# A fused projection's start: scale weights in two halves, the second half's rows behind the third chunk, more turns of the unit matrix

## What is computed

```python
def modulation(cond, w_mod, b_mod):
    m = jax.nn.silu(cond) @ w_mod + b_mod
    shift, scale, gate = jnp.split(m, 3, axis=-1)
    return shift, scale, gate

# reference
shift, scale, gate = modulation(c, w_mod[l], b_mod[l])
shift_c, scale_c, gate_c = modulation(c_ctx, w_mod[l], b_mod[l])
h = rmsnorm(x, norm_g[l]) * (1 + scale[:, None]) + shift[:, None]
hc = rmsnorm(ctx, norm_g[l]) * (1 + scale_c) + shift_c
p = h @ w_in[l]            # its first 768 columns are q (512), k (128), v (128)
```

## Time and profile before

| | |
|---|---|
| median of three runs | 1354.84 us |
| the profiled execution | 1355.44 us, of which the span 1353.6 us |
| PE busy | 98% |
| DVE, ACT, POOL busy | 71%, 43%, 46% |
| mean DMA rate over the span | 105 GB/s |
| first projection matmul | 21.42 us |

### The profile page before, as it was taken

How to read it: one execution, slowest core, us unless ns; L and a number is a source line. 1 busy time by engine, 2 the same in 40 slices (tenths; PEclk the granted TensorE clock), 3 DMA queues, 4 the chain that set the end, 5 groups by cost and what they waited for, 6 DMA issues and landing times.

```text
span 1353.6 us, 22599 instructions
## 1 busy us (share of the span) xinstructions
PE 1328.2 (98%) x7798; PEld 901.0 (67%) x7798; DVE 960.4 (71%) x1463; ACT 586.0 (43%) x1118; POOL 625.7 (46%) x314
## 2 busy tenths in 40 slices
PE   7999999999999999999999999999999999999998
PEld 5789775555555555555555554688888788878886
DVE  3598878877787777787787787542233745999986
ACT  3565335445445445445445447241313132333332
POOL 0443239998888899888888885100000010000000
PEclk9999999999999999999999999999999999999999
DMA  9867445111110111111101110943434066424431
GB/s 362 289 183 214 123 137 161 39 32 29 37 31 29 37 32 31 37 31 30 36 31 31 35 31 5 291 152 109 132 140 151 21 218 233 141 93 156 154 126 63
DMA packets 77287, 142.64 MB, mean 105 GB/s; under 512 B 7581, under 2 KB 42533, under 8 KB 75818
## 3 DMA queue, kind: packets, MB, share of 16 engines
q1 hardware_dynamic: 68746, 124.89, 28.1%
q0 software_dynamic: 7760, 16.78, 4.4%
q10 hardware_dynamic: 720, 0.15, 0.1%
HBM read 112.30 MB, written 29.50 MB: 105 GB/s over the span
## 4 chain that ended last, share of the span: by engine, by line
PE 85%; DVE 5%; issue 1%; ACT 1%; DMA 1%; SPq 0%; DVEq 0%; POOL 0%; POOLq 0%; ACTq 0%
PE pv_ps L1637 18%; PE ring_ps L1621 10%; PE ring_ps L1622 9%; PE acc L63 8%; PE acc L64 8%; PE acc L65 8%; PE ring_ps L1565 6%; PE o_ps L63 2%; PE o_ps L64 2%; PE o_ps L65 2%; PE q_ps L63 1%; PE q_ps L65 1%; PE q_ps L64 1%; PE ring_ps L1645 1%; DVE y L2294 1%
## 5 line engine op out<-in xcount | busy, mean ns | idle before, releaser
L1347 POOL TENSOR_TENSOR prob_sum<-prob_sum,prob 128x1024 f32<-128x1024 f32 x217 | 528.1, 2434 | 83.9 <-DVE prob_sum L1472 60.9
L1451 DVE TENSOR_REDUCE chunk_max<-ring_ps 128x1 f32<-128x512 f32 x496 | 307.4, 681 | 84.4 <-PE ring_ps L1565 83.2
L1386 ACT ACTIVATE prob<-ring_ps 128x512 f32<-128x512 f32 x576 | 290.0, 634 | 70.9 <-PE ring_ps L1622 70.6
L1637 PE MATMUL pv_ps<-prob,v 128*32 128x512 f32 x2304 | 260.7, 595 | 0.2 <-DVE att L1467 0.2
L1621 PE MATMUL ring_ps<-blk_q_hilo,k_hi 128*128 128x512 f32 x576 | 234.5, 407 | 2.6 <-ACT prob L1386 1.8
L1622 PE MATMUL ring_ps<-blk_q_negm,k_lo 68*128 68x512 f32 x576 | 227.6, 395 | 0.0
L1637 PEld LDWEIGHTS pv_ps<-prob,v 128*32 128x32 f32 x2304 | 68.2, 109 | 150.0 <-issue 134.1
L63 PE MATMUL acc<-hh,w_rest_hi 128*128 128x512 f32 x384 | 151.1, 394 | 0.7 <-DVE hl L98 0.7
L64 PE MATMUL acc<-hl,w_rest_hi 128*128 128x512 f32 x384 | 150.4, 392 | 0.0
L65 PE MATMUL acc<-hh,w_rest_lo 128*128 128x512 f32 x384 | 150.3, 391 | 0.0
L1621 PEld LDWEIGHTS ring_ps<-blk_q_hilo,k_hi 128*128 128x128 f32 x576 | 109.5, 190 | 51.4 <-DVE blk_q_negm L1233 13.8
(11 more groups left out here) (386 smaller groups left out, 2225.2 us busy)
## 6 DMA issues: line engine op xcount, KB each, us to landing
xt_raw<-in_xt SPq DMA_DIRECT2D x16, 512.0 KB, 5.2
x_tok<-in_x SPq DMA_DIRECT2D x16, 512.0 KB, 5.3
blk_q_max<-q_scratch SPq DMA_DIRECT2D x64, 128.0 KB, 2.6
blk_q_hilo<-q_scratch SPq DMA_DIRECT2D x32, 256.0 KB, 2.7
h_raw<-in_xg SPq DMA_DIRECT2D x4, 2048.0 KB, 8.7
rest_scratch<-stage SPq DMA_DIRECT2D x32, 256.0 KB, 2.3
rows<-in_x SPq DMA_DIRECT2D x16, 512.0 KB, 4.2
out_x<-rows SPq DMA_DIRECT2D x15, 512.0 KB, 2.6
```

The lines of the kernel that those rows point to most:

```text
L1347: nc.gpsimd.tensor_tensor(acc_pool[slot][:], acc_pool[slot][:], prob[j][:], ALU.add).then_inc(s_psum, 1)
L1386: nc.scalar.activation(prob[j][:, e * QB:(e + 1) * QB], score_bank(t)[:], ACT.Exp).then_inc(s_exp, 1)
L1451: nc.vector.reduce_max(chunk_max[:, q, c:c + 1], ring[banks[c]][:], X_AXIS).then_inc(s_mfree, 1)
L1637: last = nc.tensor.matmul(pv_ps[row:row + QUAD], k.v[:, 2 * j + e, kvh, half * QUAD:(half + 1) * QUAD], prob[j][:, e * QB:(e + 1) * QB], s ...
```

## The change

The scale weights come in two halves of 512 columns each (`w_scale[0]`, `w_scale[1]`), that is the scale of chunks 0 to 3 and of chunks 4 to 7. They lie where the shift weights will lie later, and no longer under the raw weights, so weight loads wait for nothing and the shift loads wait for the rows of the half that they overwrite. The half `b` takes two loads of 1 MB (four chunks of 512 columns each). Its rows (`scale_rows(b)`) are 32 matmuls of 128 columns, its turn is one, and `scale_columns(b)` makes four chunks' scale columns. The first half is made at the start, with nine turns of the unit matrix between its two bursts; the three turns ahead of the first turn of rows go. The second half's rows stand behind chunk 2, its turn behind tile 0's part of chunk 3, its columns on VectorE between the low parts of chunks 3 and 4 and ahead of the second halves of the x parts. Shift rows of pairs 0 and 1 stand behind chunk 6, those of pairs 2 and 3 behind chunk 7. Tile 2's x columns are loaded ahead of shift loads 2 and 3.

The diff, with the bodies of the shift rows' turn and columns left out, which do what they did:

```diff
--- before.py
+++ after.py
@@ -234,7 +234,8 @@
         b_part = place("b_part", [P, W], F32, work_at)
-        w_scale = place("w_mod_scale", [P, KD, D], F32, k.key_at)
+        w_scale = [place("w_mod_scale0", [P, KD, D // 2], F32, k.value_at),
+                   place("w_mod_scale1", [P, KD, D // 2], F32, AT_CTX_W)]
         w_raw = place("wqkv_raw", [P, KD, W], F32, k.key_at)
@@ -256,6 +257,7 @@
         row_ps = mod_ps[0]
+        scale_ps = (mod_ps[0], trq_ps)
         q_negm0, q_max0, chunk_max, neg_max = k.q_negm[0], k.q_max[0], k.chunk_max, k.neg_max
@@ -266,7 +268,7 @@
-        s_pad, s_cond, s_used = S("cond_pad_zeroed"), S("cond_ready"), S("w_scale_used")
+        s_pad, s_cond = S("cond_pad_zeroed"), S("cond_ready")
         s_mrow, s_mrow_sb, s_cols = S("mod_and_bias_rows_done"), S("mod_rows_copied"), S("mod_cols_done")
@@ -311,14 +313,11 @@
             def load_shift(i):
-                sp.wait_ge(s_used, 3)
-                if i == 3:
-                    sp.wait_ge(s_mrow, 1)
+                sp.wait_ge(s_mrow, i // 2 + 1)
                 sp.dma_start(w_shift[i // 2][:, i % 2 * 2:i % 2 * 2 + 2, :],
             def load_w(c):
-                sp.wait_ge(s_used, (1, 1, 2, 2, 2, 3, 3, 3)[c])
                 sp.dma_start(w_raw[:, c, :], w_in_v[:, c, 0:W]).then_inc(s_wr[c], 16)
@@ -338,30 +337,37 @@
 
-            for i in range(4):
-                sp.dma_start(w_scale[:, 2 * i:2 * i + 2, :], w_mod_v[:, 2 * i:2 * i + 2, D:2 * D]).then_inc(s_mod[i], 16)
+            def load_scale(i):
+                b, half = divmod(i, 2)
+                part = slice(half * KD // 2, (half + 1) * KD // 2)
+                sp.dma_start(w_scale[b][:, part, :],
+                             w_mod_v[:, part, D + b * (D // 2):D + (b + 1) * (D // 2)]).then_inc(s_mod[i], 16)
+
+            load_scale(0)
+            load_scale(1)
             load_xt(0)
+            load_w(0)
             load_xt(1)
-            for c in range(4):
+            load_w(1)
+            load_w(2)
+            load_scale(2)
+            load_scale(3)
+            for c in range(3, KD):
                 load_w(c)
             load_shift(0)
-            load_w(4)
-            load_w(5)
             load_shift(1)
-            load_w(6)
-            load_w(7)
+            load_xt(2)
             load_shift(2)
...
             load_x(1)
-            load_xt(2)
             load_xt(3)
...
                 load_x(m)
-            sp.wait_ge(s_mrow, 2)
+            sp.wait_ge(s_mrow, 3)
             sp.dma_start(c_raw[:], w_in_v[:, :, ATTN_W:W]).then_inc(s_wc, 16)
@@ -543,27 +549,31 @@
             act.wait_ge(s_mrow, 1)
-            nc.scalar.activation(mod_row[0][:], mod_ps[0][:, 0:256], ACT.Copy).then_inc(s_mrow_sb, 1)
-            for m in range(2):
-                x_high(m, slice(0, 4))
+            nc.scalar.activation(mod_row[0][:, 0:P], scale_ps[0][:, 0:P], ACT.Copy).then_inc(s_mrow_sb, 1)
+            x_high(0, slice(0, 4))
             act.wait_ge(s_scale, 2)
             w_high(0)
-            w_high(1)
+            x_high(1, slice(0, 4))
+            for c in range(1, 4):
+                w_high(c)
             for m in range(2):
                 x_high(m, slice(4, 8))
-            for c in range(2, KD):
+            act.wait_ge(s_mrow, 2)
+            nc.scalar.activation(mod_row[0][:, P:2 * P], scale_ps[1][:, 0:P], ACT.Copy).then_inc(s_mrow_sb, 1)
+            act.wait_ge(s_scale, 4)
+            for c in range(4, KD):
                 w_high(c)
-            act.wait_ge(s_mrow, 2)
+            act.wait_ge(s_mrow, 3)
             nc.scalar.activation(mod_row[1][:], mod_ps[1][:, 0:256], ACT.Copy).then_inc(s_mrow_sb, 1)
             x_high(2)
-            act.wait_ge(s_mrow, 3)
+            act.wait_ge(s_mrow, 4)
             nc.scalar.activation(b_part[:, 0:512], trq_ps[:], ACT.Copy)
-            act.wait_ge(s_mrow, 4)
+            act.wait_ge(s_mrow, 5)
             nc.scalar.activation(b_row[:, 0:512], trq_ps[0:SDK, :], ACT.Copy).then_inc(s_browhi, 1)
@@ -832,32 +842,43 @@
 
-            def mod_columns(out, i, bias):
-                cols = mod_ps[i][:, 256:512].rearrange("p (f i r) -> p f i r", f=2, i=4)
+            def scale_columns(b):
+                dve.wait_ge(s_cols, b + 1)
+                cols = scale_ps[b][:, 256:256 + P].rearrange("p (i r) -> p i r", i=4)
+                part = slice(b * KD // 2, (b + 1) * KD // 2)
                 for side in range(2):
-                    last = nc.vector.tensor_tensor(out[:, side, :].rearrange("p (i f) -> p f i", f=2),
+                    last = nc.vector.tensor_tensor(k.scale[:, side, part], cols[:, :, side],
+                                                   vecs[:, 3 * KD + b * KD // 2:3 * KD + (b + 1) * KD // 2], ALU.add)
+                last.then_inc(s_scale, 1)
+                dve.wait_ge(s_scale, 2 * b + 1)
+                gains_of = vecs[:, 4 * KD + b * KD // 2:4 * KD + (b + 1) * KD // 2]
+                nc.vector.scalar_tensor_tensor(k.scale[:, :, part], k.scale[:, :, part], 1.0,
+                                               gains_of.unsqueeze(1).broadcast_to([P, 2, KD // 2]), ALU.add,
+                                               ALU.mult).then_inc(s_scale, 1)
+
...
 
-            dve.wait_ge(s_cols, 1)
-            mod_columns(k.scale, 0, 3).then_inc(s_scale, 1)
-            dve.wait_ge(s_scale, 1)
-            nc.vector.scalar_tensor_tensor(k.scale[:], k.scale[:], 1.0,
-                                           vecs[:, 4 * KD:5 * KD].unsqueeze(1).broadcast_to([P, 2, KD]), ALU.add,
-                                           ALU.mult).then_inc(s_scale, 1)
-            for m in range(2):
-                x_low(m, slice(0, 4))
+            scale_columns(0)
+            x_low(0, slice(0, 4))
             dve.wait_ge(s_scale, 2)
             w_low(0)
-            w_low(1)
+            x_low(1, slice(0, 4))
+            for c in range(1, 4):
+                w_low(c)
+            scale_columns(1)
             for m in range(2):
                 x_low(m, slice(4, 8))
-            for c in range(2, KD):
+            dve.wait_ge(s_scale, 4)
+            for c in range(4, KD):
                 w_low(c)
-            dve.wait_ge(s_cols, 2)
-            mod_columns(k.shift, 1, 2).then_inc(s_shift, 1)
+            dve.wait_ge(s_cols, 3)
+            shift_columns().then_inc(s_shift, 1)
             dve.wait_ge(s_shift, 1)
@@ -949,24 +970,42 @@
 
-            def mod_rows(i, w, c, cw):
-                for j in range(4):
-                    last = nc.tensor.matmul(mod_ps[i][32 * j:32 * (j + 1), 0:256], cond_pad[:, c, :],
-                                            w[:, cw, j * 256:(j + 1) * 256], start=(c == 0), stop=(c == KD - 1))
-                return last
-
-            def mod_turn(i):
-                pe.wait_ge(s_mrow_sb, i + 1)
+            def keep_running(count):
+                for i in range(count):
+                    nc.tensor.transpose(trk_ps[:, 0:P], k.ident[:], k.ident[:])
+
+            def scale_rows(b):
+                for c in range(KD):
+                    if c % (KD // 2) == 0:
+                        if b == 0 and c:
+                            pe.wait_ge(s_const, 32)
+                            keep_running(9)
+                        pe.wait_ge(s_mod[2 * b + c // (KD // 2)], 16)
+                    for j in range(4):
+                        last = nc.tensor.matmul(scale_ps[b][32 * j:32 * (j + 1), 0:P], cond_pad[:, c, :],
+                                                w_scale[b][:, c, j * P:(j + 1) * P], start=(c == 0), stop=(c == KD - 1))
+                last.then_inc(s_mrow, 1)
+
+            def scale_turn(b):
+                pe.wait_ge(s_mrow_sb, b + 1)
+                nc.tensor.transpose(scale_ps[b][:, 256:256 + P], mod_row[0][:, b * P:(b + 1) * P],
+                                    k.ident[:]).then_inc(s_cols, 1)
+
...
@@ -1009,33 +1048,26 @@
             pe.wait_ge(s_cond, 1)
-            for i in range(4):
-                pe.wait_ge(s_mod[i], 16)
-                for c in (2 * i, 2 * i + 1):
-                    last = mod_rows(0, w_scale, c, c)
-                last.then_inc(s_used if i < 3 else s_mrow, 1)
-            def keep_running(count):
-                for i in range(count):
-                    nc.tensor.transpose(trk_ps[:, 0:P], k.ident[:], k.ident[:])
-
-            pe.wait_ge(s_const, 32)
-            keep_running(3)
-            mod_turn(0)
+            scale_rows(0)
+            scale_turn(0)
             keep_running(13)
             for c in range(KD):
-                if c % 4 == 0:
-                    pe.wait_ge(s_xlo, 2 + c // 2)
                 pe.wait_ge(s_wlo, c + 2 if c else 1)
                 for n in range(2):
+                    if c % 4 == 0:
+                        pe.wait_ge(s_xlo, n + 1 + c // 2)
                     q_chunk(n, c)
...
                     kv_chunk(n, c)
-                if c == 5:
+                    if c == 3 and n == 0:
+                        scale_turn(1)
```

(44 more changed lines are left out.)

## The result

| | before | after |
|---|---|---|
| median of 21 runs each | 1358.46 us | 1360.72 us |
| lowest | 1354.59 | 1357.08 |
| ratio to before | | 1.0025 [1.0017, 1.0034] |
| profiled execution (span) | 1355.44 (1353.6) | 1361.35 (1359.5) |

The change makes the kernel slower by 0.25%, about 3.4 us by the ratio (by its interval 2.3 to 4.6). One of the 21 runs after took 2632.81 us and is left out of the ratio; the median of the other 20 is 1360.46. The 3.4 us lie within the 0.3% named in the prediction, and the measured time lies outside its range, 1352.8 to 1357.2. The kernel before also reads higher over 21 runs than over the three shown at first: 1358.46 against 1354.84. So 3.6 us of the miss in absolute time are the baseline. With it even an unchanged kernel would have come out above the range.

The account below looks back on a forecast made before the run. TensorE, 98% busy, bounds the kernel. Chunk 0's 6.0 us gain goes to loads and stalls: T 0.8 later; chunk 7 ahead saves 1.6, the second chain eats 0.7: -0.1, so 1354.7 us, range 1352.8 to 1357.2.

Parts of the forecast that it names:

- the 0.3% named in the prediction: Whole kernel: 4.06 us, about what a measurement tells from no change; slower by more 0.04, faster by more 0.02.
- T: Start: moment when all shift rows are done, 40.21 us before, forecast 41.0, 0.8 later.
- rival (a): Chunks 0 to 2 and 4: low clock, 4.24 instead of 2.12 us a chunk; ends 1356.3 or 1358.4 us; chance 0.16.
- chunk 3 lands at 22.3: Loads at the start: weight chunk 3 lands at 21.9 plus 0.1 for each of four short-row loads.
- the two loads of the second half: DMA queue ahead of weight chunk 3: 5.16 us at 407 GB/s, plus 0.1 each for short rows.
- My bound for the four loads: Scale weight loads with 2 KB rows: nothing to +1.0 us on chunk 3's landing at 21.9.
- rival (c): Start: short rows at bound or second half's rows 3.9 us; tile 2 +0.6 to +1.2 us, 1355.7; chance 0.10.
- handed on one for one: Behind 46 us: all hangs on PE's progress, so the start's gain or cost reaches the end unchanged.
- Taken off the median of 1354.84: Whole kernel: the 0.1 us gain subtracted from the median before gives 1354.7 us.
- their bound: Short-row scale loads: 0.25 us more per 1024 KB, from context weights with 1 KB rows at 371 GB/s.
- (b): Second half's chain or PE's stall shorter: tile 2 at 44, -2.0 us, 1352.8; chance 0.12.

Follow-up runs that it names:

- Experiment 2: The changed kernel with weight chunk 3 loaded ahead of both scale loads of the second half; 1358.44 us, ratio 1.0015 to the kernel before.
- 11: The changed kernel with all three reordering edits, plus twenty turns of the unit matrix ahead of tile 2; 1359.52 us, ratio 1.0014 to the kernel before.
- 3: The changed kernel with the second half's rows copied ahead of the second x parts and turned ahead of chunk 3; 1357.54 us, ratio 1.0006 to before.
- 5: The changed kernel with three edits: weight chunk 3 loaded first, second half's turn first, tile 2's parts first; 1356.28 us, ratio 0.9999 to before.
- experiment 8: The changed kernel without the nine turns between the two bursts of the first half; 1360.84 us, ratio 1.0025 to the kernel before.
- experiment 1: The changed kernel again, no edit; 1360.01 us, ratio 1.0026 to the kernel before.
- experiment 12: The kernel before again, no edit; 1356.23 us, ratio 0.9998 to its other runs.
- experiment 7: The kernel before with each scale load cut into two of 512 columns (2 KB rows), same order; one execution, profiled run 1360.12 us.
- 9: The kernel before with ten turns of the unit matrix ahead of tile 2; 1359.15 us, ratio 1.0016 to the kernel before.
- 10: The kernel before with twenty turns of the unit matrix ahead of tile 2; 1360.87 us, ratio 1.0024 to the kernel before.
- 6: The changed kernel with turns of the unit matrix (16 and 13) filling PE's idle time ahead of chunks 3 and 4; 1359.26 us, ratio 1.0020 to before.
- 4: The changed kernel with tile 2's high part between the squares and its low part ahead of the variance; 1359.95 us, ratio 1.0022 to before.

## Why the prediction went wrong

**Right, by its own steps.** Chunk 0 was earlier by 6.7 us (forecast 6.0) and loads took it back. Chunk 3 was released by its low part, PE idled 1.6 us ahead of chunk 4 (2) and 0.67 ahead of tile 2 (0.7), released by the low part of x. From T to tile 2 it took 47.08 - 42.09 = 4.99 us (4.95). From chunk 3's start to chunk 4's it took 4.08 us (4.15), and to T 42.09 - 25.46 = 16.63 (16.65). Chunk 0 ran at the upper level, so rival (a) in the form in which I stated it, a clock that is low in the chunks, didn't come about. That chunk 0 was earlier than forecast is luck in part: in this profile the second burst of scale rows was already at the upper level, and where it wasn't (experiments 2 and 11) chunk 0 started at 15.4 and 15.7 us. The traces speak for turns that count as work: in three profiles (after, 3 and 5) the clock rose at 10.43, 10.61 and 9.99 us, when PE had done one burst and then only the nine turns, while in the old start one burst and a gap were followed by three more bursts before it rose, during turns. The Trainium skill, "TensorE: Matmul & The Clock Gate", Part 4: PE-mode transpose, has it that a transpose doesn't count as PE being busy; these rises disagree with it, while experiment 8 by itself decides nothing.

**The failed step: "chunk 3 lands at 22.3".** It landed at 23.4 (23.2 to 23.5 in the six profiles with this order of loads). Every later instant is late by this amount: chunk 3 by 1.11, T by 1.09, tile 2 by 1.13. Experiment 2 moves weight chunk 3 out from behind the two scale loads (it lands at 16.95) and gives back 1.2 us at 65 us, which shows the cause. The term of the sum that was mis-sized is that of the two loads of the second half, 5.16 us and 0.2 for their short rows: they took 6.29 us. The first half's second load accounts for the other 0.2 us (10.67 where I had 10.26 and 0.2). Short rows explain little: 1 MB took 2.70 us in steady running where I had 2.68, so 5.4 for the two. The other 0.9 us is a load that lands late by itself. In after the third load landed 3.66 us behind weight chunk 2 (19.79 against 16.13) and the fourth 2.63 behind it, in experiment 1 the third took 2.69 us and the fourth 3.69. In all nine profiles with the new start one of the two took 2.6 to 2.7 us and the other 3.1 to 4.0, the third in five of them, and the fourth in four. The DMA engines weren't idle meanwhile: 393 GB/s over the 7.27 us between the landings of weight chunks 2 and 3 are 2.86 MB, and the three loads that landed hold 2.49. The bytes weren't extra ones either, since both kernels had moved the same 15.87 MB when `cos_k`, the next table in the queue, landed, at 42.79 us before and at 43.46 after. So bytes of later loads went ahead while one load waited for its last part. The old order has such a load too: its second shift load took 2.95 us instead of 2.56 (3.27 in experiment 12), where nobody waited for it. What holds the load up is open. My bound for the four loads was +1.0 on 21.9; measured is +1.5, beyond it. The times are those of rival (c), which I had given 0.10.

**The second failed step: "handed on one for one".** It was read off the busy share, and PE 100% busy from 110 to 205 us does hand a delay on: 1.6 us stay 1.6. But the lag had grown from 1.05 at 46 us to 1.6 at 124 us at two waits for VectorE (0.94 us idle where before had 0.72), where the share is 51.17 of 53 us. These steps appear in the versions with the new start and not in experiments 7, 9, 10 and 12, which have the old one; why VectorE falls back there isn't shown. Beyond 207 us the executions at a clock of 0.998 and more add some 0.6 us (2.2 against 1.6). In the profiles of after and of experiments 9 and 10 that is the wait near 1120 us; it isn't shown that it is so in all.

**The baseline.** "Taken off the median of 1354.84" was a third failing: three runs, two of them at the low end of its spread, stood for a kernel whose median over 21 is 3.6 us higher. That alone put the range too low.

**Not foreseen: the clock in the attention.** Falls to half level at 209, 232 and 850 us come in some executions; the two in the profile after cost 2.5 + 1.0 us, more than the change loses at the start. They strike the old order too (experiment 7). I found no instruction of the change that causes them; filling PE's idle time (6) or not (1), and delay by itself (9: one run of 12 at 0.994; 10, 11: no run below 0.995), don't settle why the changed kernel had the lowest ones. Sorted afterwards, the clock was 0.994 or less in 11 of 64 runs of the kernels whose chunk 3 waits for the late load and whose columns come late (after, 1, 4, 6, 8) and in none of 45 of those that mend one or both of these (2, 3, 5, 11); that is a hint and no test. This part, 1.2 to 1.9 of 3.4 us, stays open, and chance isn't excluded, since experiment 1 alone had one such run in 12.

**Rivals.** The times are those of (c): chunk 3 at 25.46 (25.0 to 25.6), T at 42.09 (41.7 to 42.2), tile 2 at 47.08 (46.6 to 47.2). Neither of its two causes is, since short rows stayed below their bound (0.14 us per MB against 0.25) and the second half's rows took 1.96 us and not 3.9; that its times fit is luck. Experiment 5's start goes towards (b), 1.4 us ahead of before where (b) had 2.0: reordering can reach that. Its profile ends 0.7 us earlier than that of before, and the ratio of 0.9999 [0.9989, 1.0010] can't tell so small a gain from none.

## What to carry to other kernels

When the DMA queue is full, work brought forward on TensorE is worth nothing until the last load that the work needs is brought forward too: sum the landings first, with a margin (here one load of the queue came 0.4 to 1.3 us late), and put the small load that something waits for ahead of the large one whose user comes later. When a step is split so that half of it comes late, look in each engine's list for what stands between its last input and its first user; here two reorderings gave 0.7 to 1.8 us each. Where executions of one kernel differ by 5 us, compare them at equal granted clock and in dozens, since a baseline of three runs was 3.6 us off its own later median. And repeat a profile before a duration in it is put down to an edit: one burst took 1.08 to 1.93 us in kernels with the same TensorE instructions ahead of it.

## What the hardware showed that was not expected

- TensorE's granted clock falls to half level in a kernel whose PE is 98% busy, at recurring places (209, 232, 850 us in the profiles), in part of the executions. The stretch from 230 to 242 us read 0.72 and the lag grew there by 2.5 us. Executions of one unchanged kernel run from 1354.4 to 1359.6 us with it.
- The instant at which TensorE reaches its upper level at the start varies from profile to profile: 10.43 and 10.93 us for two of one kernel, 10.0 to 14.2 us over eight that have the same instructions on it up to there. In three of them it came when only turns of the unit matrix had run since the first burst, so turns don't keep it from rising.
- Rows of 2 KB instead of 4 KB cost 0.14 us for each MB once the queue runs steadily (2.70 against 2.56 us); the first 2 MB of the kernel landed 0.73 us later (experiment 7).
- Between the landings of weight chunks 2 and 3 (7.27 us) 393 GB/s moved 2.86 MB, while the three loads that landed hold 2.49 MB: the queue runs ahead with later loads while one load waits for its last part. A landing is thus later than the bytes ahead of it say, and which of two loads it strikes changes from one execution to the next.
